# Moving the query casts of the dilated and banded heads to GpSimd in a hybrid attention layer

## The reference

```
oa, _ = banded_attention(qa * scale, ka, va, A_WINDOW - 1, sink)
for (win, dil) in ((128, 1), (512, 4), (2048, 16)):
    qs = to_strided(qb * scale, dil)[:, :, :, None, :]
    o, lse = banded_attention(qs, to_strided(kb, dil), to_strided(vb, dil), win // dil, None)
wts = jax.nn.softmax(jnp.stack(lses, axis=0), axis=0)
ob = jnp.sum(wts[..., None] * jnp.stack(outs, axis=0), axis=0)
oc = softmax(qc * scale @ mk) @ mv
y = jnp.concatenate([oa * silu(ga), ob * silu(gb), oc * silu(gc)], axis=-1) @ w_out
h = h + rms_norm(y, post_norm)
```

## Time and profile before

| | us |
| --- | --- |
| median of 3 runs | 2151.43 (2144.21 to 2152.7) |
| the profiled execution's own time | 2152.24 |
| its span, first to last instruction | 2150.1 |
| PE busy | 2040.4 (95%) |
| PEld busy | 1717.2 (80%) |
| DVE busy | 1559.2 (73%) |
| ACT busy | 1352.9 (63%) |
| POOL busy | 115.9 (5%) |

### The profile page before, as it was taken

How to read it: one execution, slowest core, us unless ns; L and a number is a source line. 1 busy time by engine, 2 the same in 40 slices (tenths; PEclk the granted TensorE clock), 3 DMA queues, 4 the chain that set the end, 5 groups by cost and what they waited for, 6 DMA issues and landing times. The chain is left out here.

```text
span 2150.1 us, 39340 instructions
## 1 busy us (share of the span) xinstructions
PE 2040.4 (95%) x12892; PEld 1717.2 (80%) x12892; DVE 1559.2 (73%) x4410; ACT 1352.9 (63%) x3520; POOL 115.9 (5%) x116
## 2 busy tenths in 40 slices
PE   5999999999999999999889999999999998899998
PEld 4787778888888888888778888887888887688886
DVE  6564674546654574436589999989799997888886
ACT  7454454544555464343699999989699997533333
POOL 1232310000000000002100000000000000000000
PEclk7999999999999999999889999999999999999999
DMA  4466576777577667588876687686779895345543
GB/s 158 152 229 222 177 242 180 217 247 217 155 223 212 225 196 235 184 286 272 201 148 138 130 167 143 131 161 139 150 184 220 227 249 171 98 164 168 176 160 113
DMA packets 351736, 401.40 MB, mean 187 GB/s; under 512 B 105616, under 2 KB 255248, under 8 KB 346688
## 3 DMA queue, kind: packets, MB, share of 16 engines
q1 hardware_dynamic: 343120, 364.80, 62.0%
q0 software_dynamic: 8432, 34.30, 5.2%
HBM read 255.62 MB, written 143.39 MB: 186 GB/s over the span
## 5 line engine op out<-in xcount | busy, mean ns | idle before, releaser
L854 PE MATMUL p_ps<-p_u_hi,p_w_hi 128*128 128x512 f32 x1344 | 534.0, 397 | 26.7 <-DVE p_p_c L739 10.8
L856 PE MATMUL p_ps<-p_u_hi,p_w_lo 128*128 128x512 f32 x1344 | 526.6, 392 | 0.0
L855 PE MATMUL p_ps<-p_u_lo,p_w_hi 128*128 128x512 f32 x1344 | 525.6, 391 | 0.0
L570 DVE TENSOR_TENSOR p_w_lo<-p_w_raw,p_w_hi 128x512 fp32r<-128x512 f32 x336 | 246.6, 734 | 327.0 <-ACT p_w_hi L423 325.4
L1621 ACT ACTIVATE probs<-probs,a_stat 128x256 f32<-128x256 f32 (+1 forms) x896 | 437.4, 497 | 38.9 <-DVE a_stat L1455 36.5
L423 ACT ACTIVATE p_w_hi<-p_w_raw 128x512 fp32r<-128x512 f32 x336 | 211.2, 629 | 329.0 <-PE p_ps L856 304.7
L854 PEld LDWEIGHTS p_ps<-p_u_hi,p_w_hi 128*128 128x128 f32 x1344 | 254.2, 189 | 85.4 <-issue 13.0
L856 PEld LDWEIGHTS p_ps<-p_u_hi,p_w_lo 128*128 128x128 f32 x1344 | 253.7, 189 | 54.4
L855 PEld LDWEIGHTS p_ps<-p_u_lo,p_w_hi 128*128 128x128 f32 x1344 | 254.2, 189 | 50.8
L1455 DVE CUSTOM_DVE_ANT_0 probs<-a_ps_s,fixed 128x256 f32<-128x256 f32 (+1 forms) x704 | 251.9, 398 | 48.3 <-PE a_ps_s L1354 45.7
L1424 PE MATMUL a_ps_t<-fixed,probs 128*128 128x128 f32 x1660 | 262.0, 279 | 23.6 <-ACT a_pT L1645 16.5
(11 more groups left out here) (202 smaller groups left out, 2762.6 us busy)
## 6 DMA issues: line engine op xcount, KB each, us to landing
p_w_raw<-in_w_in SPq DMA_DIRECT2D x156, 256.0 KB, 3.7
p_w_raw<-scratch_w_s SPq DMA_DIRECT2D x144, 256.0 KB, 3.6
scratch_qk_hi<-p_out_a SPq DMA_DIRECT2D x80, 256.0 KB, 4.0
scratch_qk_lo<-p_out_b SPq DMA_DIRECT2D x80, 256.0 KB, 4.1
a_v<-scratch_v SPq DMA_DIRECT2D x40, 512.0 KB, 8.2
scratch_gate<-p_out_a SPq DMA_DIRECT2D x64, 256.0 KB, 3.8
scratch_v<-p_out_a SPq DMA_DIRECT2D x256, 64.0 KB, 2.3
a_gate<-scratch_gate SPq DMA_DIRECT2D x64, 256.0 KB, 6.0
```

What stands on the lines that cost most here:

```text
L570: nc.vector.tensor_tensor(w_lo[:, m % 3, :, :], w_raw[:, entry(j, g), :, :], w_hi[:, m % 3, :, :].bitcast(F32), ALU.subtract).then_inc(w_l ...
L854: nc.tensor.matmul(bank, hi, u_hi[j][:, k, :], start=j < 2 and k == 0, stop=False, skip_group_check=True)
L855: nc.tensor.matmul(bank, hi, u_lo[j][:, k, :], start=False, stop=False, skip_group_check=True)
L856: last = nc.tensor.matmul(bank, lo, u_hi[j][:, k, :], start=False, stop=k == KH - 1, skip_group_check=True)
```

## The change

POOL gets a part of its own in the rounds. For B, from the second phase on, it waits until the phase's queries are loaded and until PE has made the last scores of the phase before, and then makes all eight casts in a row: four into place 1 and four into place 2. For A it waits until the next phase's queries are loaded and the place is free, and makes the four casts in a row. In A's first round it makes the casts of the first two phases. The casts have the same shapes and patterns as before. ACT's and DVE's casts go, with the waits in front of them. The waits of PE and of SP are unchanged. POOL's transfers of L1919 and L1925 now stand behind its casts.

```diff
--- before.py
+++ after.py
@@ -1097,8 +1097,6 @@
 
 
     heads = {"A": 6, "B": 6, "C": 4}[kind]
-    Q_SLOTS = {1: 0, 3: 1, 5: 2, 7: 3}
-    N_SLOTS = {2: 0, 4: 1, 6: 2, 8: 3}
     Q_ORDER = {8: 1, 9: 2, 10: 3, 11: 4}
     q_row = {"A": QA, "B": QB, "C": QC}[kind]
     y_row = {"A": 0, "B": 384, "C": 768}[kind]
@@ -1281,20 +1279,6 @@
                 sp.dma_start(stored_half(sc["y"], h, s, g), gate[g * HD:(g + 1) * HD, s, :]).then_inc(y_stored[s], 16)
 
         return named(store=store, q=load_q, k=load_k, v=load_v, gate=load_gate, mask=load_mask, memory=load_memory)
-
-    def copy_natural(eng, phase, slot, copy):
-
-
-        n = number(phase)
-        for p, first in ((0, 1), (1, 10)) if n == 0 else ((n + 1, 2),):
-            if first <= slot < first + 2 and p < 2 * heads:
-                if slot == first:
-                    eng.wait_ge(q_loaded, 32 * p + 32)
-                    if p < 2:
-                        eng.wait_ge(prev.scores_ready, prev.TOTAL)
-                    else:
-                        eng.wait_ge(scores_ready, (p - 1) * NP)
-                copy(p, slot - first)
 
     def natural_piece(g):
 
@@ -1544,17 +1528,6 @@
                 last = nc.vector.tensor_scalar(place, place, coef[:, s, u.column:u.column + 1], None, ALU.mult)
             last.then_inc(weighted, 1)
 
-        def copy_queries(phase, slot):
-            p = number(phase)
-            if kind == "B" and slot in N_SLOTS and p > 0:
-                if N_SLOTS[slot] == 0:
-                    dve.wait_ge(q_loaded, 32 * p)
-                    dve.wait_ge(scores_ready, p * NP)
-                nc.vector.tensor_copy(*natural_piece(N_SLOTS[slot])).then_inc(natural_copied, 1)
-            if kind == "A":
-                copy_natural(dve, phase, slot, lambda p, g: nc.vector.tensor_copy(
-                    *natural_part(p, 2 + g)).then_inc(q_copied, 1))
-
         def finish(phase, d):
             if last_of.get(d, -1) >= MERGED:
                 finish_bank(phase, d, last_of[d] - MERGED)
@@ -1607,7 +1580,7 @@
             dve.wait_ge(bank_read, number(phase) * NC + c + 1)
             by = gate[:, s, :].rearrange("p (u r a) -> p u r a", u=4, a=HD)[:, :, :, 32 * c:32 * c + 32]
             nc.vector.tensor_tensor(by, summed.rearrange("p u (r a) -> p u r a", a=32), by, ALU.mult).then_inc(y_ready, 1)
-        return named(scores=scores, exchange=exchange if kind == "B" else inverse, scale=scale, finish=finish, finish_rest=finish_rest, gated=gated, copy_queries=copy_queries)
+        return named(scores=scores, exchange=exchange if kind == "B" else inverse, scale=scale, finish=finish, finish_rest=finish_rest, gated=gated)
 
     def scalar_parts(act):
 
@@ -1657,29 +1630,37 @@
             ge(act, bank_read, p * NC)
             nc.scalar.activation(y16[:, 4 * g:4 * g + 4, :], ps_o[:, g % 2, :].rearrange("p (u n) -> p u n", n=P),
                                  ACT.Copy).then_inc(kept, 1)
-        def copy_queries(phase, slot):
-            if kind == "A":
-                copy_natural(act, phase, slot, lambda p, g: nc.scalar.activation(
-                    *natural_part(p, g), ACT.Copy).then_inc(q_copied, 1))
+        return named(scores=scores, exchange=exchange, copy=copy, keep=keep)
+
+    def pool_parts(pool):
+
+        def cast(phase):
             p = number(phase)
-            if kind != "B" or slot not in Q_SLOTS or isinstance(p, int) and p == 0:
-                return
-            i = Q_SLOTS[slot]
-            if i == 0:
-                act.wait_ge(scores_ready, p * NP)
-                act.wait_ge(q_loaded, 32 * p)
-            by = by_residue(q[:, 0, :])
-            to = q[:, 1, i * CHUNK:(i + 1) * CHUNK].rearrange("p (b i a) -> p b i a", i=4, a=8)
-            of = by[:, 4 * i:4 * i + 4, :].rearrange("p i (b a) -> p b i a", a=8)
-            nc.scalar.activation(to, of.bitcast(F32), ACT.Copy).then_inc(q_copied, 1)
-        return named(scores=scores, exchange=exchange, copy=copy, keep=keep, copy_queries=copy_queries)
+            if kind == "B" and p > 0:
+                pool.wait_ge(q_loaded, 32 * p)
+                pool.wait_ge(scores_ready, p * NP)
+                for i in range(4):
+                    nc.gpsimd.tensor_copy(q[:, 1, i * CHUNK:(i + 1) * CHUNK].rearrange("p (b i a) -> p b i a", i=4, a=8),
+                                          by_residue(q[:, 0, :])[:, 4 * i:4 * i + 4, :].rearrange(
+                                              "p i (b a) -> p b i a", a=8).bitcast(F32)).then_inc(q_copied, 1)
+                for g in range(4):
+                    nc.gpsimd.tensor_copy(*natural_piece(g)).then_inc(natural_copied, 1)
+            if kind == "A" and p < 2 * heads:
+                pool.wait_ge(q_loaded, 32 * p + 32)
+                if p < 2:
+                    pool.wait_ge(prev.scores_ready, prev.TOTAL)
+                else:
+                    pool.wait_ge(scores_ready, (p - 1) * NP)
+                for g in range(4):
+                    nc.gpsimd.tensor_copy(*natural_part(p, g)).then_inc(q_copied, 1)
+        return named(cast=cast)
 
     return named(
         kind=kind, heads=heads, phases=2 * heads, NP=NP, NS=NS, TAIL=TAIL, EARLY=EARLY, TOTAL=TOTAL,
         scores_ready=scores_ready, values_done=values_done, max_ready=max_ready, turned=turned,
         turned_copied=turned_copied, bank_read=bank_read, coef_ready=coef_ready, done_sem=done_sem, y_stored=y_stored,
         q_copied=q_copied, copied_by=copied_by, natural_copied=natural_copied,
-        loads=loads, tensor_parts=tensor_parts, vector_parts=vector_parts, scalar_parts=scalar_parts)
+        loads=loads, tensor_parts=tensor_parts, vector_parts=vector_parts, scalar_parts=scalar_parts, pool_parts=pool_parts)
 
 
 def load_y(sp, sc, ahead, i, b, rows=(0, KD // 2)):
@@ -1763,8 +1744,6 @@
                     x.parts.scale(x.phase, e)
                 for v in slot.new:
                     a.parts.scores(a.phase, v)
-                if a:
-                    a.parts.copy_queries(a.phase, i)
                 if slot.three_before:
                     x, e = slot.three_before
                     x.parts.finish(x.phase, e)
@@ -1789,8 +1768,15 @@
                     x.parts.keep(x.phase, e)
                 for v in slot.new:
                     a.parts.scores(a.phase, v)
-                if a:
-                    a.parts.copy_queries(a.phase, i)
+
+        def pool_round(a, c, b, d):
+            if a and a.g.kind == "B":
+                a.parts.cast(a.phase)
+            elif a and a.g.kind == "A":
+                n = 2 * a.phase[0] + a.phase[1]
+                if n == 0:
+                    a.parts.cast((0, 0))
+                a.parts.cast(((n + 1) // 2, (n + 1) % 2))
 
         def rounds(eng, round_, parts_of):
 
@@ -1925,6 +1911,7 @@
                     pool.dma_start((ahead.b11, ahead.b21, ahead.b22)[n], io["w_out"][rows * P:(rows + half) * P, at:at + CHUNK].rearrange(
                         "(k p) n -> p k n", p=P)).then_inc(ahead.w_loaded, 16)
 
+                rounds(pool, pool_round, lambda g: g.pool_parts(pool))
                 for n in range(4):
                     pool.wait_ge(A.done_sem, (9 + n) * NC)
                     load_sum(n)
```

## The result

The changed kernel takes 2170.68 us, median of four runs (2168.01 to 2175.22), against 2148.57 us of four runs before (2144.21 to 2152.7). The ratio is 1.0105, 95% interval 1.0074 to 1.0137. The profiled execution took 2168.01 us, 15.8 us more than the one before; its span is 2166.2 us, 16.1 us more. The forecast was 2152 us, "no change". The time lies in the wide range (2131 to 2176 us), but outside the forecast's own (2142 to 2163). In the experiments one run of e4_filler, of 11215 us, is left out.

What follows compares the result with a forecast made beforehand. It took DVE as the bound at B's change of round and throughout A, ACT in B's following slots. First B round -2.1, ten B rounds 0.0 each, ten A rounds +0.3 each: +0.9 us, no change, 2152 us; range 2131 to 2176.

Steps and rivals of the forecast that it cites:

- wide range: Whole kernel: 2131 to 2176 us, taking in most of both large rivals; the forecast's own range was 2142 to 2163.
- second rival: B's change of round: DVE's delay is passed on to PE, 2.1 us per round, 2173 us in all; chance 0.27.
- POOL's own times: POOL's casts: 0.58 us each alone, up to 0.9 where waiting for a scale; nobody would wait for the copies.
- The scale L1544 is exposed, the scores L1455 are not: DVE beside POOL's casts: scales wait for the shared SBUF path, scores read from PSUM are free.
- first rival: POOL costs DVE next to nothing because L1544 is not exposed: -27 us, 2125 us; chance 0.25.
- The price on DVE: DVE's waits beside POOL's casts: 0.30 us a cast, 2.4 us per B round; 1.0 us per A round.
- ACT's and DVE's relief: B's rounds without their casts: 1.8 us from ACT in slots 0 to 8, 0.34 us from DVE's first cast.
- bound of -1.8: B's rounds, best case: 1.8 us shorter each when POOL costs DVE nothing.
- the pace of C: Stage C, which has no casts, runs at 1.50 us per slot; taken as the floor for slots without casts.
- The first part of a delay meets no one: B's change of round: ACT stands a little behind DVE, so 0.3 us of delay per round costs nothing.
- A: A's rounds: DVE loses 1.0 us to POOL, gains 0.68 from its casts, +0.3 us per round; first round nothing.
- B's first round: First round with casts: ACT's lost casts gain 2.1 us, with bounds of 0 and 4 us.

Runs made afterwards that it cites:

- e4_filler: Changed kernel plus four idle TensorE transposes in each of the last three slots of a B round: 2168.55 us, ratio 1.0056 to before.
- e6_no_casts: Changed kernel with each of GpSimd's casts cut to one column, waits and counts kept: 2135.07 us, ratio 0.9898 to before.
- e1 to e4: Four kernels: only B's casts on GpSimd (1.0077), only A's (1.0011), B's three slots later (0.9966), changed kernel with idle transposes (1.0056); ratios to before.
- e3_later: Changed kernel with GpSimd starting B's eight casts behind the third group of the new round's scores: 2144.99 us, ratio 0.9966 to before.
- e8_dve_late: e3_later plus one unread DVE reduction behind the scores of each of the last three slots of a B round: 2170.55 us, ratio 1.0071 to before.
- e12_b_later_again: Kernel before with only B's casts moved to GpSimd, behind the round's third group of scores; a repeat run: 2142.5 us, ratio 0.9951 to before.
- e14_later_filler: e12_b_later_again plus idle TensorE transposes only in its gaps around odd-to-even changes of round: 2140.48 us, ratio 0.9950 to before.
- e1_b_only: Kernel before with only B's casts moved to GpSimd, A's left on ACT and DVE: 2171.4 us, ratio 1.0077 to before.
- e5_more_filler: Changed kernel plus eight idle TensorE transposes in each of the last three and first four slots of B's rounds: 2183.57 us, ratio 1.0107.

## Where the prediction was right and where it missed, by its steps

The wide range was drawn around the rivals and holds the time in part by luck: its upper end rests on the second rival's price of 2.1 us in every round, which did not come, and the clock, which the prediction did not have, filled the gap.

**POOL's own times: right.** 0.6 us alone, 1.07 us at most, and nobody waited for them.

**The scale L1544 is exposed, the scores L1455 are not: right,** and so is the choice against the first rival. The trace of after shows it for this form: 1.19 us a pair against 0.48. That is as the Trainium skill's rule has it ("SBUF — State Buffer", "SBUF: two separate sides").

**The price on DVE: too high.** 2.4 us per round of B were taken; the scales lengthened by 1.4, and one gate multiplication by 0.17. Several casts passed beside the scores.

**ACT's and DVE's relief: the step that was mis-sized.** 1.8 + 0.34 us per round were taken off as relief, and 0.3 as delay that meets no one. (The bound of -1.8 and the first rival leave the 0.34 out; with it they are -2.1 per round and 3 us lower in all.) The relief measured by itself, e6_no_casts against before, is 0.25 us in even and 0.85 us in odd rounds, since PE becomes the bound. The stretch of B showed PE busy for 348 of 360 us; the pace of C, from which the floor of 1.50 us per slot was taken, is not that of B's slots. In the forecast two terms that were both too large cancelled to 0.0. The real pair is +0.9 and +1.55 us for the casts (after against e6_no_casts) less 0.25 and 0.85: +0.6 and +0.7 us per round, about 7 us in ten.

**"The first part of a delay meets no one": wrong.** Nearly all of DVE's delay came out in the round: 1.2 us of 1.4 to 1.6.

**The clock: missing from the sum, and the largest term.** A fall costs 44.2 - 39.5 = 4.7 us. Four are 19 us, less the 3.5 us of the two short ones before (1.7 each over 38.9). The nine rounds then add up to 5 x 0.6 + 4 x 0.7 + 15.3 = 21 us, as measured. The runs agree in size: the mean clock went from 0.9732 (before beside e1 to e4) to 0.9665. Over the 30 runs of before that stood beside e1 to e4, the time changes by 1.6 us for each 0.001 of clock, and over e3_later's runs by 1.9. So some 10 to 13 us of the 22 go with the clock and the rest is the direct delay. That the two estimates (15 and 10 to 13) differ is left open; the number of falls varies between runs of one kernel, and only one execution of each has a trace.

**The second rival** had the right size, 2173 us, and the right mechanism for its first part: DVE's delay at the change of round is passed on, and in e8_dve_late as well. But its price, 2.1 us in each of ten rounds, was not seen. The direct part is a third of that.

**A.** +0.3 us per round was forecast, -0.26 measured (151.6 to 148.8 over eleven). The relief of 0.68 was right (13.3 to 12.6 in e6_no_casts); POOL's price was 0.4, not 1.0. A's first round was set at nothing and grew by 2.3 us, with a clock of 0.91 against 0.95. B's first round was forecast at -2.1 and gave -2.5.

Of the theories after the result, "casts on GpSimd cost what they cost wherever they stand" fell with e3_later, and "the clock only goes with the delay" with e12_b_later_again, where a round with the same row ahead of it is 5 us longer when the clock falls. In e14_later_filler against e12_b_later_again the filling alone took the last fall away; the mean clock of twelve runs rose by 0.003, of which 0.001 is also in the runs of before beside them. Still open is why one even round falls and another doesn't: in e12_b_later_again PE was busy for 5.91 us of 7.1 without a fall and 5.78 with one, and laid 0.1 us later, as far ahead of the first exponential as the other, the first reads 5.80.

## What to carry to other kernels

Before work is moved to an engine that shares a path with a busy one, ask in which slots the busy one waits, and start the moved work there: B's casts on GpSimd made the kernel 0.8% slower at one place and 0.5% faster three slots later (e1_b_only and e12_b_later_again). Where TensorE is 95% busy on average, read the granted clock by short stretches, above all at changes of round; a delay of 1 to 2 us on another engine can cost a fall of the clock, worth more than the delay. Don't count the relief of an engine in full when the next one is 97% busy.

## What the runs showed of the hardware that I had not expected

- A granted clock of 1.00 can fall to 0.50 (1.2 GHz) in the middle of a stage with PE 95% busy, for 6.8 to 17 us at a time in these kernels; ahead of it PE was busy for 5.15 of 7.1 us (after). A round of 39.5 us became one of 44.2. Its matmuls are then slower while it looks fully busy (13.22 of 13.60 us), so PE's busy share is high just where time is lost.
- Idle transposes in PE's gaps kept the clock at 1.00 through nine rounds in the two profiles that had them there. In e5_more_filler they cost 2 to 4 us a round, more than the falls; in e14_later_filler next to nothing, 0.0 us in eight of nine rounds and 1.5 us in one.
- A pair of float32 scales of 128 by 128 in SBUF on DVE takes 1.19 to 1.25 us beside GpSimd's casts and 0.48 alone; the scores read from PSUM are not touched (420 against 421 ns).
